# A two-layer hybrid decoder step: three cache copies and the first latent scores moved ahead, page gathers released inside the scores

## What is computed

```python
past_s = dict(..., ckv=cache_mla_ckv[l][page_table].reshape(db, past_len, KV_LORA),
              krope=cache_mla_krope[l][page_table].reshape(db, past_len, DROPE))
s = jnp.einsum('bqhc,blc->bhql', ql, ckv_all) + jnp.einsum('bqhr,blr->bhql', qr, krope_all)
p = jax.nn.softmax(jnp.where(key_rows[None, :] <= rows[:, None], s * scale, -jnp.inf), axis=-1)
o_lat = jnp.einsum('bhql,blc->bqhc', p, ckv_all)          # then through kv_up to yc
m = gates[0] * (ya @ w_a) + gates[1] * (yb @ w_b) + gates[2] * (yc @ w_c)
new_state = dict(swa_k=k_all[:, -keep:], swa_v=v_all[:, -keep:], ...)
```

## Time and profile before

| | us |
|---|---|
| median of three runs | 2611.89 |
| the three runs | 2611.89, 2600.38, 2613.0 |
| the profiled execution, its own time | 2601.21 |
| span of the profiled execution | 2599.4 |
| PE busy in it | 2524.6 (97%) |
| DVE, ACT, POOL busy | 1312.9 (51%), 563.0 (22%), 67.5 (3%) |
| granted TensorE clock, mean | 0.992 of full speed |

### The profile page before, as it was taken

The page is one execution under the profiler, slowest core; times in us unless marked ns, Lnnn a source line. Parts: engine busy times, 40 slices in busy tenths (PEclk is TensorE's granted clock), DMA queues, the critical chain, the costliest instruction groups (busy, mean ns, idle before and its releaser), DMA issues.

```text
span 2599.4 us, 52968 instructions
## 1 busy us (share of the span) xinstructions
PE 2524.6 (97%) x23108; PEld 2054.2 (79%) x23108; DVE 1312.9 (51%) x2839; ACT 563.0 (22%) x1257; POOL 67.5 (3%) x92
## 2 busy tenths in 40 slices
PE   7999999999999999999999999999999999999998
PEld 6999856656666667999999998566666566689998
DVE  5663553335543472665376535533455335627654
ACT  2110231133432221201021102311344222221011
POOL 0000000000000110000000000000000001100000
PEclk9999999999999999999999999999999999999999
DMA  6435668643971479544444457686439433894443
GB/s 232 150 113 145 227 230 325 227 150 119 385 274 65 144 259 368 158 130 120 141 153 130 122 152 249 236 317 212 175 148 391 182 119 124 299 341 142 130 112 87
DMA packets 260709, 505.66 MB, mean 195 GB/s; under 512 B 9792, under 2 KB 198720, under 8 KB 245376
## 3 DMA queue, kind: packets, MB, share of 16 engines
q1 hardware_dynamic: 251776, 330.83, 38.6%
q0 software_dynamic: 8704, 171.45, 18.0%
HBM read 491.95 MB, written 140.85 MB: 243 GB/s over the span
## 4 chain that ended last, share of the span: by engine, by line
PE 91%; DMA 3%; ACT 2%; DVE 2%; issue 1%; PEld 1%; SPq 0%; DVEq 0%; ACTq 0%
PE ps L719 86%; PE ps L722 5%; DMA big<-in_cache_swa_k_dram 1%; DMA big<-in_w_branch_c_dram 1%; PEld ps L719 1%; ACT big L1858 1%; ACT reg L1858 0%; DMA ring<-in_f_wu_dram 0%; DVE reg L2024 0%; DVE reg L2098 0%; DVE x L2016 0%; DVE reg L2616 0%; DVE ring L2537 0%; DVE reg L2587 0%; ACT big L1608 0%
## 5 line engine op out<-in xcount | busy, mean ns | idle before, releaser
L719 PE MATMUL ps<-reg 128*128 128x160 f32 (+12 forms) x4584 | 515.7, 293 | 4.1 <-issue 2.5
L719 PEld LDWEIGHTS ps<-reg 128*128 128x128 f32 (+5 forms) x4584 | 455.0, 163 | 37.4 <-issue 27.6
L719 PE MATMUL ps<-h,ring 128*128 128x320 f32 (+2 forms) x1984 | 447.7, 377 | 14.3 <-DMA ring<-in_f_wu_dram 13.3
L719 PE MATMUL ps<-reg,ring 128*128 128x160 f32 (+1 forms) x3040 | 458.9, 306 | 0.0
L719 PEld LDWEIGHTS ps<-reg,ring 128*128 128x128 f32 x3040 | 426.1, 189 | 16.4 <-issue 6.2
L719 PEld LDWEIGHTS ps<-h,ring 128*128 128x128 f32 (+1 forms) x1984 | 322.5, 189 | 104.2 <-issue 25.4
L719 PE MATMUL ps<-ring,h 128*128 128x512 f32 (+3 forms) x896 | 249.4, 470 | 1.2 <-issue 1.2
L719 PEld LDWEIGHTS ps<-big,ring 128*128 128x128 f32 (+2 forms) x2016 | 197.6, 168 | 28.7 <-issue 24.4
L719 PE MATMUL ps<-big,ring 128*128 128x160 f32 (+2 forms) x2016 | 215.1, 279 | 4.1 <-issue 3.6
L719 PEld LDWEIGHTS ps<-ring,h 128*128 128x128 f32 (+1 forms) x896 | 102.0, 163 | 78.0 <-issue 62.5
L719 PE MATMUL ps<-big,reg 32*64 32x256 f32 (+8 forms) x2144 | 134.7, 348 | 5.1 <-issue 5.1
(11 more groups left out here) (323 smaller groups left out, 2664.8 us busy)
## 6 DMA issues: line engine op xcount, KB each, us to landing
out_o_swa_k_s_dram<-in_cache_swa_k_dram POOLq DMA_DIRECT2D x16, 4080.0 KB, 16.0
out_o_swa_v_s_dram<-in_cache_swa_v_dram POOLq DMA_DIRECT2D x16, 4080.0 KB, 16.6
ring<-in_w_in_dram SPq DMA_DIRECT2D x30, 2048.0 KB, 8.6
ring<-in_f_wd_dram SPq DMA_DIRECT2D x32, 1408.0 KB, 7.0
ring<-in_f_wg_dram SPq DMA_DIRECT2D x42, 1024.0 KB, 5.5
ring<-in_f_wu_dram SPq DMA_DIRECT2D x42, 1024.0 KB, 8.1
big<-in_cache_swa_k_dram SPq DMA_DIRECT2D x32, 1024.0 KB, 8.5
ring<-in_cache_swa_v_dram SPq DMA_DIRECT2D x32, 1024.0 KB, 7.3
```

What stands on the lines that cost most here:

```text
L719: return pe.matmul(out, lhsT, rhs, start=first, stop=last, skip_group_check=True)
```

## The change

- The copies: `COPY_AT` becomes (3, 11, 14). Copies 11, 12 and 13 of a layer are issued behind the gather of sample 0 and ahead of that of sample 1. The last two are issued when all scores are done (`ml_mm` at 2·NB), behind the last gather. SP waits for copy 14 before it clears semaphores in the second feed-forward block.
- The first scores: `own_tokens(0)` and `scores(0)` leave `ml_sample` and are handed to `prompt` as `ahead`, where PE runs them behind `values(7)` and ahead of the last seven dealt steps. The exponentials of sample 0 stand on ACT ahead of the last gate tile. The wait for gate tile 24 moves to `shares(0, 1)`, that for tile 23 to `own_tokens(1)`. The own tokens of sample 0 use bank 4 instead of 6. DVE takes the own scores of sample 1 behind the low keys and the own share of sample 0 instead of ahead of them.
- The gathers: `ml_mm` is raised twice for each sample, at the end of depth piece 5 and of piece 8. The gathers of samples 3 to 7 wait for piece 5 of the scores of sample b - 2. The gather of sample 2 waits for all of the scores of sample 0, and only its second half of latents for the last gate product. From sample 4 on the rotary keys are issued ahead of time, behind the latents of the sample before.
- The third and fourth set of buffers exchange places, so `ring` at 0 to 4607 now belongs to samples 3 and 7 instead of 2 and 6, and the load that takes slot 0 next waits for the values of sample 7 instead of 6.

```diff
-COPY_AT = (3, 11)
+COPY_AT = (3, 11, 14)
+OWN_BANK = (4, 6)
...
-        kr_at = [(big, 3072, big, 5120, big, 7168), (reg, 10720, reg, 12768, reg, 14816), (ring, 0, ring, 2048, ring, 4096),
-                 (ring, 9088, h_flat, 0, h_flat, 2048)]
+        kr_at = [(big, 3072, big, 5120, big, 7168), (reg, 10720, reg, 12768, reg, 14816), (ring, 9088, h_flat, 0, ring, 11136),
+                 (ring, 0, ring, 2048, ring, 4096)]
...
                 for b in range(NB):
                     if b == 0:
                         pool.wait_ge(S["sws_done"], NB)
                     elif b == 1:
+                        copied(COPY_AT[1], COPY_AT[2])
                         pool.wait_ge(S["prompt_mm"], 2 * H + 16)
                         pool.wait_ge(S["ml_prep"], 1)
                     elif b in (2, 3):
                         pool.wait_ge(S["prompt_y"], 2 * H)
                         pool.wait_ge(S["ml_prep"], 1)
-                        pool.wait_ge(S["pgm"], 24)
-                        pool.wait_ge(S["ml_mm"], b - 1)
+                        pool.wait_ge(S["ml_mm"], b)
                     else:
                         pool.wait_ge(S["ml_pv"], b - 3)
-                        pool.wait_ge(S["ml_mm"], b - 1)
...
+                        pool.wait_ge(S["ml_mm"], 2 * (b - 2) + 1)
+                    if b < 4:
+                        krope_gathered(b)
                     for half in range(2):
...
-                copied(COPY_AT[1], 2 * NB)
+                        if (b, half) == (2, 1):
+                            pool.wait_ge(S["pgm"], 24)
+                        latents_gathered(b, half)
+                    if 3 <= b < NB - 1:
+                        krope_gathered(b + 1)
+                pool.wait_ge(S["ml_mm"], 2 * NB)
+                copied(COPY_AT[2], 2 * NB)
...
                 left = cap - begun[0]
                 deal(left // 2, cap)
                 values(7)
+                if ahead:
+                    ahead()
                 deal(left, cap)
...
+                    if d in (5, 8):
+                        q.then_inc(S["ml_mm"], 1)
...
+            def first_ml_scores():
+                pe.wait_ge(S["ml_prep"], 1)
+                pe.wait_ge(s_ql, 16 * 12)
+                ml_own_tokens(0)
+                ml_scores(0)
...
-                prompt("mlp", scores, vrow, N_DEAL)
+                prompt("mlp", scores, vrow, N_DEAL, first_ml_scores)
...
                 prompt("mlp", lambda r, w: Sp[r][:, 0, 0:w], SCC, yc, N_DEAL)
+                ml_exponentials(0)
                 gates_out(24)
...
                 for b in range(NB):
                     maximum(b)
-                    own_scores(b + 1)
+                    if b:
+                        own_scores(b + 1)
                     keys(b + 1, 0)
                     if b >= 2:
                         result(b - 2)
                     own_share(b)
+                    if b == 0:
+                        own_scores(1)
                     keys(b + 1, 1)
                     divisor(b)
```

More of the change, by code:

```diff
@@ L1162, in bc_proj, with prompt @@
                         deal(DEAL_QK // 8)
-            def prompt(tag, scores, rows, cap):
+            def prompt(tag, scores, rows, cap, ahead=None):
                 base = PROMPT0[tag]
@@ L1465, in shares @@
                             pe.wait_ge(S["ml_osb"], b)
+                        else:
+                            pe.wait_ge(S["gate"], 24)
                         q = tr(ps[0:NS, 7, 448:512], PnL, NS)
@@ L1926, in ml_sample @@
                 for b in range(NB):
-                    exponentials(b)
+                    if b:
+                        ml_exponentials(b)
                     output(b - 1)
```

102 lines of the change are left out of this document (52 added, 50 removed).

## The result

The changed kernel takes 2580.92 us (median of four runs, 2569.88 to 2582.86), the kernel before 2606.48 beside it: a ratio of 0.9884, interval 0.985 to 0.9917, so 1.2% faster. The profiled execution took 2582.86 us. The forecast was 2586 in a range of 2570 to 2604.

What follows compares the result with a forecast made beforehand. PE bounds the kernel, busy 2524.6 of 2599.4 us. Gains 9.6 + 7.7 + 5.2 − 2.1 = 20.4 us took 2601.2 to 2580.8; adding 5.4, half the gap between run levels, gave 2586 us, range 2570 to 2604.

Steps and rivals of the forecast that it cites:

- First scores: Samples' latent attention: first scores ahead of the last seven dealt steps remove idle time and slow clock behind it, 9.6 us.
- the slack: At the first scores: dealt steps and own tokens cover the 3.46 us chain of maximum and exponentials with about 1 us spare.
- rival of the first wait coming back: PE waits at the first transposes again, 7.7 of the 9.6 us stay, gain 12.7 us; chance 0.12.
- Copies away from the last scores: Last sample's stretch: without copies beside branch c's weights, idle time and slow clock go, 7.7 us of at most 9.5.
- The one wait of 1.8 us: Last sample's stretch: one wait of the smallest size seen, left in the sum because branch c's weights still load there.
- Gathers released inside the scores: Three too long middle stretches: gathers end about 1.4 us earlier, idle times shrink; 5.2 us, the middle of 0 and 10.4.
- got its turn when the gather was through: Layer 0's 16.84 us stretch: PE's idle time read as an instruction transfer held until the gather ended.
- Three copies in the prompt's part: About 768 to 820 us: late PE instructions and branch b's weights cost 2.1 us for two layers.
- rival that "issue" has nothing to do with gathers and copies: PE's waits without a visible cause are unrelated to these transfers; only 7.5 us gained, 2594 or 2599 us; chance 0.22.
- Slower by copies in the prompt's part: 768 to 820 us: copies starve PE, 6.3 us a stall; three stalls a layer make it 15 us slower; chance 0.06.
- The half level of 5.4 us: Whole kernel: runs lie on two equally frequent levels, the median 10.7 us above the profiled execution; half is added.
- my sentence that an idle time of more than 2 us costs clock: Samples' attention: idle times over 2 us slow PE's clock, while one of 1.69 us left it at 1.00.

Runs made afterwards that it cites:

- small gathers: The changed kernel with the latent gathers of samples 2 to 7 bringing 16 of 128 rows: 2578.5 us, ratio 0.9898 to the kernel before.
- small copies: The changed kernel with the eight cache copies beside the recurrence in each layer moving 16 of 240 parts: 2572.63 us, ratio 0.9866 to the kernel before.
- the first group: Four kernels on one chip: copies alone, first scores alone, gathers alone, and changed kernel with gather of sample 3 later; kernel before beside them 2609.78 us.
- the first two groups: The first four kernels, then four variants (gathers cut, copies cut, copies in feed-forward block, copies' change undone), each group on its chip; kernel before 2609.78 and 2606.58 us.

## Why the prediction was right, point by point

The forecast lay 5.1 us above the time. Its base, 2601.2 + 5.4 = 2606.6, met the 2606.48 that the kernel before took beside it, so the miss is that of the gain: 25.6 us between medians, where the sum had 20.4.

- **First scores, 9.6 us.** By program position the profile gained 5.7 and 5.65 us there, 11.4; alone the part measured 0.49%, 12.8 us (8.1 to 17.5). The mechanism was right at each point: the wait for the exponentials is gone, the slack was enough, the stretch behind it at full clock. The first scores' own edit does not give all of it: alone it left the stretch behind at 12.18 and 12.39 us, some 4.5 us more than here. The earlier gather of sample 2 may be what gives them back; no run takes that apart. It came out larger because the stretch behind the first scores took 10.10 and 9.99 us, not the 10.57 of a later sample that I had set for it, and PE's work in the first some 0.3 us less. The rival of the first wait coming back is out.
- **Copies away from the last scores, 7.7 us.** Measured by its stretches 6.40 + 4.11 = 10.5. The one wait of 1.8 us that I left in place for branch c's weights didn't come, and a last sample, which has no own tokens, takes 10.1 and 10.0 us and not 10.57. This term was sized too small; alone the part gave 0.60%, 15.7 us (10.4 to 20.6), net of its price in the prompt's part.
- **Gathers released inside the scores, 5.2 us.** Measured 3.9 − 0.9 = 3.0 us in the profile, 3.7 (−1.3 to 8.9) alone, the latter with the late maximum in it. The middle between 0 and 10.4 came near by two errors that met, which is luck. The step that was wrong in it is that each stop would stay and become 1.4 us shorter. The stops at the samples further on went altogether, and at sample 2, where the gathers of samples 2 and 3 and the rotary keys of sample 4 now run one into the next, there is one in each layer: new in layer 0, and in layer 1 at the same place of the grid as before, with more slow clock behind it (10.24 us for 3.41). My reading that the transfer "got its turn when the gather was through" fits these rows: the transfer for row 8161 lands at 907.65 us as the gathers run out, as in the earlier trace rows and in the kernel with the gather of sample 3 later. Single microseconds there, in the changed kernel:

```profile
906.00:907.00 1.00, 0.69 (x25) 0.20 (x9) 0.83 (x6) 0.00 (x0) 0.00 (x0) 1.00 0.82 328
907.00:908.00 1.00, 0.00 (x0) 0.00 (x0) 0.14 (x1) 0.00 (x0) 0.64 (x1) 1.00 0.16 61
```

  It is no rule for every transfer. The next one moved from 912.48 to 913.43 us in the middle of gathers:

```profile
912.00:913.00 1.00, 1.00 (x12) 0.71 (x10) 0.88 (x5) 0.48 (x1) 0.00 (x0) 1.00 1.07 369
914.00:915.00 1.00, 1.00 (x12) 0.52 (x8) 1.00 (x1) 0.01 (x1) 0.00 (x0) 1.00 0.99 414
```

  What lets one through and holds another stays open. Whether a late one hurts depends on how short PE's block is.

- **Three copies in the prompt's part, −2.1 us.** PE lost nothing between 768 and 820 us, and the weights of branch b came in time. So this term measured 0; a spell of slow clock in layer 1 (below) is not its doing. The reason I gave for the low price, fewer instructions per us, is right in kind: a block lasts PE 27 to 33 us there.
- **The rival that "issue" has nothing to do with gathers and copies (0.22)** is out: with small gathers the stops go from the samples, with small copies from the recurrence. In the changed kernel's profile the crossing of a block cost PE nothing that shows where a block lasts 17 us or more, in the feed-forward part and between 768 and 820 us, and up to 2.59 us where PE had spent 5.2 to 7.0 us on it.
- **Slower by copies in the prompt's part (0.06)** didn't come with three or four copies. It did come with five, through weights and not through instructions. That was the wrong mechanism for a right fear.
- **The half level of 5.4 us.** I had taken the two levels as a property of the kernel to be split. The 25 executions of the kernel before in the first group lie from 2595.92 to 2616.31 us around 2609.78 and show no two equally frequent levels, so the half was right by luck. A good part of that range is likely the copies beside the recurrence: its length differs by up to 8 us in a layer from one profile to another. The profiled execution after was a long one in this respect, the one before a short one in layer 1, which hid 7.2 us of the gain.

## What to carry to other kernels

Look at where the stops under "issue" stand in the program as well as in time: if they are a multiple of one number of instructions apart and each follows the landing of an instruction transfer, suspect late blocks of instructions, and try to keep bulk transfers away from where PE runs through its program fastest. Bulk copies are not free under long matmuls either: beside weight loads they made these four times slower (34.6 us to landing for 8.0), so a place for a copy must be free of late instructions and of weights that are due. Cost a stretch from more than one execution when copies run beside it, as a difference of 7 us lay in a part that no edit touched. And before parts that were measured apart are added up, see in their profiles that they ran under the same conditions; here a maximum that was taken late, worth up to some 10 us, stood in some and not in others.

## What the runs showed of the hardware

- **The late maximum.** In the profiles of the first two groups with early release, DVE began the maximum late behind the last score matmul, mostly by 1.6 to 2.5 us and three times by 0.8 to 0.9, in samples 1 to 5, where POOL began to issue a gather less than half a microsecond ahead of it or was at it. In the other profiles it came after 0.2 us at most, in the changed kernel at the same distance. It costs some 1.1 us a sample (11.7 us for 10.57). It went by the group and so by the chip: it stands in all six profiles of two chips, and in none of the four others with early release. That it is a property of the chip is a guess that no run tests: no kernel with early release is known to have run on chips of both kinds. It means that the measured gain of the gathers alone (first group) may be low by up to some 10 us.
- **Slow clock without idle time.** In layer 1 the clock stood at 0.50 of full speed from 2095.66 to 2099.08 us with PE busy throughout, behind 32 matmuls of 64x64. It is there (0.94 on average from 2080 to 2110) with the copies' change undone too, so it doesn't come from the copies, and absent when the changed kernel ran again. Three stretches of it:

```profile
2095.00:2096.00 1.00, 1.00 (x5) 0.68 (x5) 0.00 (x0) 0.77 (x2) 0.00 (x0) 0.83 0.00 0
2096.00:2099.00 3.00, 3.00 (x10) 2.18 (x9) 1.07 (x7) 1.48 (x5) 0.00 (x0) 0.50 0.00 0
2099.00:2100.00 1.00, 1.00 (x5) 0.73 (x4) 0.74 (x3) 0.25 (x2) 0.00 (x0) 0.96 0.05 16
```

- **The price of one stop.** The stop at sample 2 was 2.23 us in layer 0, where the clock stayed at 1.00, and 2.10 us in layer 1, where 10.24 us at 0.50 came behind it: 2.75 against 7.6 us in all. In a second execution neither stop (2.61 and 1.96 us) had slow clock behind it. So my sentence that an idle time of more than 2 us costs clock, which fits the stretches before (2.48 and 2.53 us idle at mean clocks of 0.80 and 0.89, 1.69 at 1.00), doesn't hold for each. What decides which comes I can't tell from these rows.
- **Unequal shares.** Beside a copy, weight loads took four times as long (34.6 us for 8.0). In ten microseconds of the kernel with copies in the feed-forward block, 130 to 140 us, both a copy and a weight load are under way (packets, MB, and the share, in which packets that reach past the end count whole):

```profile
q0 software_dynamic: 61, 3.98, 105.8%
q1 hardware_dynamic: 173, 0.18, 5.2%
```

The copy's packets have 65,280 bytes and take 2.9 us each, the load's 1,024 bytes and 0.05 us. The engines moved 2.8 of the small ones for each large one (173 for 61), and the load got 4% of the bytes. Whether copies in smaller parts would leave it more wasn't tried. An instruction transfer is one packet of 16,384 bytes. If it has to wait for a copy's packet on its engine, it is late by up to 2.9 us; that is an estimate from the time of such a packet, beside the median of 3.8 us under full DMA engines. The gathers' packets have 8,192 bytes and take 0.31 us, so this doesn't explain the stops beside gathers.
